# Sigmoid into SBUF, a mask inside the scan, work issued by readiness: a two-layer stick-breaking encoder on eight cores

## The reference, cut to what matters

```python
h = rms_norm(x, norm1_g)
q, k, v, u, gate_pre = split(h @ w_in)               # 512, 512, 512, 512, 2048
g_pool, g_sb = split(sigmoid(gate_pre + b_gate))
a = pool_mixer(u)            # trailing means over 2/4/8/16 tokens, minus the token, 4 small maps
s = stick_breaking_attention(q, k, v)                # 8 heads of 64
x = x + (g_pool * (a @ w_branch_pool) + g_sb * (s @ w_branch_sb)) @ w_out
gt, up = split(rms_norm(x, norm2_g) @ w_ffn_in)      # 2 x 2816
x = x + (silu(gt) * up) @ w_ffn_out
```

## Time and profile before

| | us |
|---|---|
| median of 3 runs | 2545.31 (2544.48 to 2701.86) |
| the profiled execution's own time | 2533.05 |
| its span, slowest core (4) | 2531.5 (cores 2512.6 to 2531.5) |
| PE busy | 2133.5 (84%), 11096 matmuls |
| DVE busy | 1146.3 (45%) |
| POOL busy | 954.7 (38%) |
| ACT busy | 862.7 (34%) |
| mean granted TensorE clock | 0.925 of 2.4 GHz |

### The profile page before, as it was taken

One profiled execution on the slowest core, in us unless ns is written; L12 is line 12 of the kernel. 1 busy time (PEld: TensorE's weight loads), 2 busy tenths in 40 slices (PEclk: granted clock), 3 DMA queues, 4 the chain that ended last, 5 costly groups with the idle time before them and its releaser, 6 DMA issues.

```text
span 2531.5 us, 38757 instructions; the slowest of 8 cores (2512.6 to 2531.5 us)
## 1 busy us (share of the span) xinstructions
PE 2133.5 (84%) x11096; PEld 991.0 (39%) x11096; DVE 1146.3 (45%) x1394; ACT 862.7 (34%) x1497; POOL 954.7 (38%) x969
## 2 busy tenths in 40 slices
PE   1888689857788989898899989996888995989994
PEld 0433244423344654333344434332333342434441
DVE  1144667766466231465322225876566431242222
ACT  2344444434332323443322235444332323221011
POOL 0123566634555411464233205763665510310010
PEclk9988689978999999898999999998999998999997
DMA  5536566835456455676344547875575644444442
GB/s 120 117 54 131 90 98 104 145 65 73 76 90 102 79 110 94 126 117 108 59 79 76 104 92 147 133 130 77 98 106 97 104 82 126 75 75 82 81 74 72
DMA packets 384605, 244.79 MB, mean 97 GB/s; under 512 B 333072, under 2 KB 336144, under 8 KB 384400
## 3 DMA queue, kind: packets, MB, share of 16 engines
q0 software_dynamic: 41520, 120.29, 29.5%
q1 hardware_dynamic: 342880, 122.03, 25.0%
HBM read 265.95 MB, written 16.84 MB: 112 GB/s over the span
## 4 chain that ended last, share of the span: by engine, by line
PE 58%; DMA 14%; DVE 10%; issue 6%; ACT 5%; POOL 5%; SPq 1%; DVEq 0%; POOLq 0%; ACTq 0%
PE psb L308 58%; DMA WT<-W 10%; DVE E L462 6%; POOL W L297 3%; DVE H L301 2%; DMA yT<-X 2%; ACT psb L290 2%; DMA X<-xA 1%; POOL STG L297 1%; ACT H L290 1%; SPq L480 1%; DVE X L297 1%; ACT L290 1%; ACT RS L290 1%; DVE RA L297 0%
## 5 line engine op out<-in xcount | busy, mean ns | idle before, releaser
L308 PE MATMUL psb<-H,WR 128*128 128x512 bf16 (+2 forms) x4960 | 1023.6, 363 | 50.3 <-DVE RA L297 49.4
L297 POOL TENSOR_TENSOR W<-E 128x768 bf16<-128x768 f32 (+6 forms) x456 | 553.9, 1220 | 662.5 <-DVE E L462 300.2
L308 PEld LDWEIGHTS psb<-H,WR 128*128 128x128 bf16 x4960 | 480.9, 100 | 540.1 <-issue 105.2
L462 DVE TENSOR_TENSOR_SCAN E<-psb,ZF 128x770 f32<-128x770 f32 (+10 forms) x264 | 375.8, 1431 | 368.1 <-ACT psb L290 308.4
L308 PE MATMUL psb<-RA,WR 128*128 128x512 bf16 (+2 forms) x2160 | 447.5, 365 | 9.9 <-POOL RA L297 4.8
L290 ACT ACTIVATE psb<-psb 128x770 f32<-128x770 f32 (+6 forms) x456 | 303.4, 675 | 294.1 <-PE psb L308 236.3
L346 POOL DMA_DIRECT2D WR<-weights x280 | 155.6, 559 | 624.4 <-PE psb L308 606.7
L290 ACT ACTIVATE STG<-psb 128x512 f32<-128x512 f32 (+2 forms) x352 | 175.2, 543 | 515.0 <-PE psb L308 460.7
L462 DVE TENSOR_TENSOR_SCAN E<-psb,CAR,ZF 128x530 f32<-128x530 f32 (+4 forms) x192 | 293.2, 1534 | 92.7 <-ACT psb L290 67.4
L297 DVE TENSOR_TENSOR RA<-STG,psb 128x512 bf16<-128x512 f32 (+2 forms) x198 | 124.6, 630 | 440.4 <-POOL STG L297 252.5
L308 PEld LDWEIGHTS psb<-RA,WR 128*128 128x128 bf16 x2160 | 210.1, 100 | 231.2 <-issue 35.3
(11 more groups left out here) (36 smaller groups left out, 825.2 us busy)
## 6 DMA issues: line engine op xcount, KB each, us to landing
WR<-weights POOLq DMA_DIRECT2D x152, 512.0 KB, 5.9
WR<-weights POOLq DMA_DIRECT2D x64, 352.0 KB, 4.8
WR<-weights POOLq DMA_DIRECT2D x64, 256.0 KB, 5.8
yT<-X SPq DMA_DIRECT2D x32, 256.0 KB, 2.4
WT<-W SPq DMA_TRANSPOSE x456, 3.1
X<-xA SPq DMA_DIRECT2D x8, 520.0 KB, 7.8
xsA<-X SPq DMA_DIRECT2D x8, 520.0 KB, 4.4
X<-xsA SPq DMA_DIRECT2D x8, 520.0 KB, 8.5
```

The lines of the kernel that those rows point to most:

```text
L297: P.op(eng, lambda e: e.tensor_tensor(out=out, in0=in0, in1=in1, op=op), reads, writes, d=(1.67 * N + 185) if eng == 'pool' else (1.05 * N ...
L308: P.op('pe', lambda e: e.matmul(out, lhsT=lhsT, rhs=rhs, start=start, stop=stop, **kw), reads, writes, inc, d=max(N, 64) / 2.4 + 6 if d is ...
L462: P.op('dve', lambda e: e.tensor_tensor_scan(out=E, data0=za, data1=zero, initial=init, op0=ALU.mult, op1=ALU.add), r_z + [('ZF', 0, 16)] ...
```

## The change

Seven edits go together. (1) The sigmoid reads each score part from one of three rotating banks (0 to 2) and writes E in SBUF; the scan runs in place on E. (2) The mask matmul and ZF go. Bank 3 holds a constant mask in bf16 for the whole run, and the scan takes it as second operand with `max`: 1 where s >= t, -1 elsewhere; units off the diagonal take one column of -1, broadcast. (3) Operations of ScalarE, VectorE and POOL, the transposes and the output stores go to a list; one is put on its queue when the planner's clock says that its inputs are there, or when a later step needs it. (4) While attention is ahead of a schedule (share of attention done against share of the dense stage done, times 0.95, less 0.02), and dense work is ready within 500 ns, attention waits. (5) Layer 0's projections go tile by tile (K, next tile's norm, V, Q), from weights loaded once into RA and STG. (6) In `rest(1,'B')` the pool outputs go to WT, and all eight rows of X are loaded at its start. (7) The planner's constant for a DMA's landing is 3400 instead of 2500 ns. Cut to its core:

```diff
+PACE = 0.95
+LEAD = 0.02
+    def pump(self):
+        go = True
+        while go:
+            go = False
+            for x in list(self.wait):
+                t = max(self.t[x['eng']], self.t['pe'])
...
+                if not bad and self.ready(x['reads'], x['writes'], before=x) <= t + 100.0:
+                    self.force(x)
+                    go = True
     def op(self, eng, fn, reads=(), writes=(), inc=True, d=100.0):
+        if eng == 'pe' or fn is None:
+            self.free(reads, writes)
+            self._op(eng, fn, reads, writes, inc, d)
+            return
+        x = dict(eng=eng, fn=fn, reads=list(reads), writes=list(writes), d=d, dma=None)
+        x['est'] = max(self.ready(reads, writes), self.t[eng]) + d
+        self.wait.append(x)
+        self.pump()
...
-        self.fin.setdefault(stream, []).append(max(self.tdma + 1800.0, t + 2500.0))
+        self.fin.setdefault(stream, []).append(max(self.tdma + 1800.0, t + 3400.0))
...
-        def pool_out(h, c, t0, t1):
+        def pool_out(l, h, c, t0, t1):
+            if (l, h) == (depth - 1, 'B'):
+                o = c * XW - R0[h]
+                return WTt[:, o + t0:o + t1], ('WT', o + t0, o + t1)
...
+        def keep_part(u, a, b_):
+            zb = cnt['z'] % 3
+            cnt['z'] += 1
+            pe(ps(zb, 0, b_ - a, 0, nq), Q.ap(hp, q0, q0 + nq, p0, p1),
+               K.ap(hp, k0 - 2 + a, k0 - 2 + b_, p0, p1), True, True, ...)
+            act(Et[0:nq, eo + a:eo + b_], ps(zb, 0, b_ - a, 0, nq), AF.Sigmoid, ..., scale=-1.0)
...
-            act(za, za, AF.Sigmoid, r_z, r_z, W, scale=-1.0)
+            low = MSK[0:nq, 0:W] if first else MSK[0:nq, NMSK:NMSK + 1].to_broadcast([nq, W])
             P.op('dve', lambda e: e.tensor_tensor_scan(
-                out=E, data0=za, data1=zero, initial=init, op0=ALU.mult, op1=ALU.add),
+                out=E, data0=E, data1=low, initial=init, op0=ALU.mult, op1=ALU.max),
...
+            win = {(0, 'B'): 'R0A', (1, 'A'): 'R0B', (1, 'B'): 'R1A'}.get((l, h))
...
+        def on_time():
+            win, part = cnt['pace']
...
+            t0, t = marks[win]
+            return (spent[0] - t0) / t >= part * PACE - LEAD
...
+        def project0(h, tiles, kbs, before):
+            for x, (t0, t1) in enumerate(tiles):
+                for kind in 'kvq':
+                    if kind == 'v':
+                        if x in before:
+                            yield from before[x]()
...
         for k, (t0, t1) in enumerate(T3):
             x_load_tile('A', 2 + k, t0, t1)
-        x_pump(True)
-        wget(0, 'A', 'k', 1)
+            x_pump(True)
+            load_static('kvq'[k], [X['A'].r(7, *T3[0])])
+            if k == 0:
+                load_mask()
...
+            if len(cand) > 1 and not on_time() and any(c[1] == 1 and c[0] <= now + 500.0 for c in cand):
+                cand = [c for c in cand if c[1] != 0]
```

More of the change, by code:

```diff
@@ L91, in needs, with _fin, ready @@
         return need
-    def ready(self, reads, writes, skip=()):
+    def _fin(self, s, v):
+        return self.fin[s][v // 16 - 1 if s.startswith('D:') else v - 1]
+    def ready(self, reads, writes, skip=(), before=None):
         t = 0.0
         for s, v in self.needs(reads, writes).items():
[L96 to L100, removed]
-        return t + 80.0
+            if s not in skip:
+                t = max(t, self._fin(s, min(v, self.cnt[s])))
+        for x in self.wait:
+            if x is before:
+                break
+            if self.clash(x, reads, writes):
+                t = max(t, x['est'])
+        return t + 80.0
@@ new lines, in _hit, with clash, force @@
+    @staticmethod
+    def _hit(a, b):
+        return any(p[0] == q[0] and p[1] < q[2] and q[1] < p[2] for p in a for q in b)
+    def clash(self, x, reads, writes):
+        return self._hit(x['writes'], reads) or self._hit(x['writes'], writes) or self._hit(x['reads'], writes)
+    def force(self, x):
+        for y in list(self.wait):
+            if y is x:
+                break
+            if y in self.wait and self.clash(y, x['reads'], x['writes']):
+                self.force(y)
+        if x in self.wait:
+            self.wait.remove(x)
+            if x['dma'] is None:
+                self._op(x['eng'], x['fn'], x['reads'], x['writes'], True, x['d'])
+            else:
+                self._dma(x['eng'], x['fn'], x['dma'], x['reads'], x['writes'], x['d'])
@@ L103, in _record, with flush @@
+    def flush(self):
+        while self.wait:
+            self.force(self.wait[0])
     def _record(self, reads, writes, stream, val, skip):
@@ L108, in _record @@
             assert v <= self.cnt.get(s, 0), ("dependency on a not-yet-issued inc", s, v)
[L109 to L120, removed]
+        for tab, rs in (('R', reads), ('W', writes)):
+            for (an, lo, hi) in rs:
+                A = self.arenas[an]
+                c0, c1 = lo // CELL, (hi + CELL - 1) // CELL
+                if stream not in A[tab]:
+                    A[tab][stream] = np.zeros(A['n'], np.int64)
+                A[tab][stream][c0:c1] = val
         return need
@@ L139, in op, with dma, _dma @@
         self.ops.append(dict(eng=eng, fn=fn, need=need, inc=inc, dma=None))
-    def dma(self, queue, fn, sem, reads=(), writes=(), d=1000.0):
+    def dma(self, queue, fn, sem, reads=(), writes=(), d=1000.0, hold=False):
+        if not hold:
+            self.free(reads, writes)
+            self._dma(queue, fn, sem, reads, writes, d)
+            return
+        x = dict(eng=queue, fn=fn, reads=list(reads), writes=list(writes), d=d, dma=sem)
+        x['est'] = max(self.ready(reads, writes), self.t[queue]) + 3500.0
+        self.wait.append(x)
+        self.pump()
+    def _dma(self, queue, fn, sem, reads, writes, d):
         stream = 'D:' + sem
@@ L749, in gate @@
                     if x == 0:
[L750 removed]
+                        src = [pool_out(l, h, c, t0, t1) for c in range(4)]
                     else:
@@ L762, in rest @@
             yield from run_order(8, tiles, 0, 0, gate, None, gfree)
-            x_load(l, h, (6, 7))
+            x_load(l, h, [n for n in range(8) if n not in low])
             def outp(n, tile):
```

181 lines of the change are left out of this document (121 added, 60 removed).

## The result

The changed kernel takes 2315.72 us in the median of four runs (2306.31 to 2609.14) against 2548.09 for the kernel before in four: the ratio is **0.907, interval 0.902 to 0.913**, some 236 us less. The forecast was 2207 with a range of 2090 to 2420, so direction and range held, and the size fell short by about 100 us.

What follows compares the result with a forecast made beforehand. The prediction saw VectorE's and GpSimd's in-order queues waiting for each other, leaving TensorE underfilled. First gate at 235, then stages of 507, 484, 552 and 415 sum to 2193 us; plus 1.5 and 12.3, 2207 us, range 2090 to 2420.

Steps and rivals of the forecast that it cites:

- the stretch up to the gates: First score matmul to first gate group: TensorE needs 135 us at full speed, at 0.78 that is 173.
- The signs: Trace marks named beforehand: right if waits fall and first gate nears 235; wrong if sigmoids wait or scans exceed 1.8 us.
- Readiness order: VectorE and GpSimd queues beside FFN: issuing ready operations first opens their mutual wait, 115 us, between 0 and 252.
- Pacing: Attention spread over the following dense stage fills norms' gaps; extra score visits cost 20 us, between 0 and 50.
- Mask: Attention scores: 256 mask matmuls go, 0.22 us each, saving TensorE 56 us.
- the rival at half rate: Attention scan pays for a second stream and takes twice as long; 2774 us, slower, 5% chance.
- Last stage: Layer 1 B: pool outputs go to WT, so the 26.07 us store wait and about 4 of slow clock go.
- Score banks: Three rotating banks, freed after ScalarE instead of the scan: 50 of TensorE's 73.6 us waiting on scans go.
- First projection by tile: Start, layer 0: first square at 27 instead of 36.13 us, first score at 62 instead of 97.35.
- The E ring: Three sigmoid buffers in attention, 1.55 us a unit, less than one scan: not binding before VectorE.
- the wait changes its name: Rival: E's buffers or ScalarE replace the VectorE-GpSimd loop, windows keep today's shares; 2408 us, 25% chance.
- It doesn't do what it says: Rival: order often wrong, attention ends late; only last stage and half the mask gain stay; 2491 us, 7% chance.

Runs made afterwards that it cites:

- E4: Changed kernel with layer 0's projections and their loads as before the change; ratio 0.909 to the kernel before.
- E6: Changed kernel with a norm's Exp queued right behind its Ln on ScalarE; 2305.35 us, ratio 0.907.
- E7: Changed kernel with X loads and stores issued from ScalarE's queue instead of SP's; 2316.08 us, ratio 0.909.
- E11: Changed kernel with four W buffers instead of three; 2308.42 us, ratio 0.908.
- E5: Kernel before with the readiness list alone, plus eight transpose semaphores instead of four and the 3400 ns landing constant; ratio 0.966.
- E9: Kernel before with readiness order and pacing, nothing else of the change; ratio 0.942, 147 us gained.
- E10: Kernel before with pacing alone; 2524.5 us, ratio 0.993.
- E2: Changed kernel without pacing, attention never held back; ratio 0.961.
- E3: Changed kernel with the mask put back as matmuls, sigmoid still to SBUF; 2384.18 us, ratio 0.938.
- E8: Changed kernel with half A's X tile borders on multiples of 16 columns, and eight transpose semaphores; 2301.9 us, ratio 0.904.
- E1: Changed kernel with every operation queued in the planner's program order, other edits kept; 2492.49 us, ratio 0.982.

## Why the prediction held, and which step was mis-sized

**The sum by stages** was 2193 us of span; core 0 has 2297.1. The 104 us are: start +4, the stretch up to the gates +63, layer 0 A +2, layer 0 B +20, layer 1 A +16, last stage -1.

**The signs.** Of those for right, the product ahead of the subtraction (in the timeline shown), the scans, the y stores and the clock of layer 0 A (0.96) came true; VectorE's wait (106.2 for under 100) just missed, and the first gate (301.7 for 235) missed by far. Of those for wrong, two came: sigmoids waiting for GpSimd's subtraction (89.4) and TensorE waiting for ScalarE (50.7).

**The step that failed is the stretch up to the gates**, 173 us at a share of 0.78. Its work was nearly right: 173.59 x 0.83 = 144 us at full clock for 135. Its share was not: 144 / 235.9 = 0.61, little above the 127 / 229.1 = 0.55 of before. The 0.78 came from no row. I took the stretch as TensorE's work over one share; it is two things, one behind the other (E4's lines): half A's attention, 212.5 us, and then 23.4 us of pool stage that had not been done beside it, with 14 units of half B in between. The first alone is longer than the 173 us. The chain of waits over the stretch, by line, and the transposes in it:

```profile
by line: PE psb L381 34.8%; DMA WT<-W 22.2%; SPq L560 10.8%; issue 9.7%; POOL W L370 5.0%; ACT H L363 3.7%; DVE E L542 3.5%; DVE H L374 2.7%; ACT E L363 1.8%; ACT L363 1.8%; SPq L470 1.0%; ACT RS L363 0.7%; SPq L238 0.6%; SPq L476 0.5%; ACT
...
L560 SPq DMA_TRANSPOSE WT<-W x102: 1086/1199/8464, 68.6 to 301.1; - x102
...
DMA to landing us min/median/max: 2.2/2.6/17.7
```

A third of the chain is transposes, landing or being issued: 1.2 us each on SP's queue in the median, 1.09 to 1.21 for the first eight, which have 16 queries and 16 keys, and 2.6 to land. But the share of transposes does not explain the length, for E4's stretch is the shortest of all and has more of it (47%, core 0):

```profile
by line: DMA WT<-W 35.5%; PE psb L381 32.7%; SPq L560 11.2%; POOL W L370 6.4%; issue 5.8%; DVE E L542 1.9%; ACT L363 1.8%; ACT H L363 1.4%; ACT E L363 1.2%; SPq L238 0.6%; POOLq L238 0.3%; ACT RS L363 0.3%; ACT STG L367 0.3%; ACTq L238 0.2%
```

Half A's 88 transposes come 2.4 us apart in the changed kernel, 2.6 before (229.1 us) and 2.2 in E4. E4 has 142 x 0.84 = 119 us of TensorE's work at full clock in its stretch, 25 less; so work moved in beside the attention went with a longer stretch, not a fuller one. What sets 2.2 to 2.6 us a unit, and what would bring the pool stage in beside the units, stays open: by the medians of the cores E6 takes 8 us from the stretch, E7 and E11 3 each, and a fourth buffer E was not tried.

**Readiness order**, 115 us (0 to 252), which entered the sum only by way of the shares: alone 87, with pacing a wait of 103.5 instead of 252.5. The mechanism was right, but I credited the order with what needs both. My reading is that two in-order queues let go of each other only when attention's units also come apart in time; that both are needed is shown (E5, E9, E10), this reason for it is not.

**Pacing** I priced by its cost, 20 us of visits, which then entered no term of the sum, and let its gain stand in the shares 0.90 and 0.93. The gain is 136 us (E2). The visits left no mark: the three long windows hold 449 + 451 + 511 = 1411 us of TensorE at full clock (busy times clock) for 456 + 450 + 513 = 1419 forecast. Their shares came out at 0.88, 0.90 and 0.90 for 0.90, 0.93 and 0.93. That layer 0 A landed within 2 us is luck: 7 us less work and the lower share cancel. The two others missed by 36 together, for 0.93 was too good; which waits take the rest there was not taken apart.

**Mask**: 56 us forecast, 43 to 51 by E3. **Scan**: unchanged, 1753 for 1758 ns, so the rival at half rate falls. **Last stage**: -30 forecast, -29.9 measured; the y stores' wait is gone. **Score banks**: TensorE no longer waits for scans (73.6 before) but 50.7 us for ScalarE, so of the 50 us that I took as gone about 23 are; E9, without the new banks, has 44.3 us of that wait left.

**First projection by tile**: 62 and 65.8 at the first score, first square 27 and 28.66, and worth nothing in the end: E4's time is the same. The wait for the second tile was seen; that the static weights read the shared cell and so hold up the next X load was priced as contention (17 us) and is an ordering: aligned borders give it back (E8). So the near hit of 27 is luck in part.

**The E ring** I held not to bind (1.55 us a unit). Its wait appeared, 89.4 us, as the thing late next. E11 cuts it to 63.7 for nothing, so that part at least is not the bound; the rest was not tested. So "the wait changes its name" happened in name, at 38 of the 169 us that this rival put on the three long windows (1581 us measured, 1543 forecast, 1712 by the rival). "It doesn't do what it says" is refuted by E1 and E2.

## What to carry to other kernels

An issue order by readiness and the spacing of the second stream are one edit: two coupled in-order queues gave 87 us for the first, 19 for the second and 147 for both. Price a stretch by what it must hold and which part ends last: here a chain of small units, 88 of them 2.2 to 2.6 us apart, and the dense work that is left when the chain is over. Work moved in and an earlier opening shortened neither. A wait that falls is no price: E10's fell by 58 us for 19 us of time, E11's by 70 for none. When an early gain vanishes (E4, E6, E7), look for the stage behind it that grew; whether pacing makes it grow was not tested.

## What was not expected of the hardware

- TensorE's records show a third clock, 0.81, on cores 6 and 7 from about 2040 to 2190 us, with TensorE always busy: 29 us of the last stage. The Trainium skill, TensorE: Matmul & The Clock Gate, Part 1, tells of a peak-current limit that takes the whole die to 13/16. The value agrees; that two cores of a die have it while cores 4 and 5 beside them stand at 1.00 does not.
- A transpose issued behind two X loads of 2 MB on SP's queue landed after 17.7 us, for a median of 2.6. With the loads on ScalarE's queue the slowest still took 12.9 us to land (E7, core 0), and TensorE's longest wait fell from 15.2 to 5.1. The Trainium skill, DMA: Bandwidth & Descriptors, Queues, rings and completion order, says that each DMA engine takes one queue's descriptors in order and that SP and ScalarE have queues of their own, on the same engines. The traces agree with both: another queue takes away some 5 of the 17.7 us.
- VectorE's scan costs the same with its second operand streamed from PSUM and the first in SBUF as with the first in PSUM and a column of zeros as second: 1753 and 1758 ns at 770 columns.
